# RWKV block products on all four 64 by 64 quarters of TensorE, with masks moved to GpSimd

## The reference

```
sa    = S @ a_t
S     = S * w_t + outer(sa, b_t) + outer(v_t, k_t)
y_t   = S @ r_t
```

## Time and profile before

| | us |
|---|---|
| median of 3 runs | 1494.84 |
| lowest and highest run | 1488.73, 1506.45 |
| profiled execution, its own time | 1494.61 |
| its span | 1492.7 |
| PE busy | 1369.0 (92%) |
| PEld busy | 1040.0 (70%) |
| DVE busy | 697.6 (47%) |
| ACT busy | 506.6 (34%) |
| POOL busy | 172.6 (12%) |

### The profile page before, as it was taken

How to read it: one execution, slowest core, us unless ns; L and a number is a source line. 1 busy time by engine, 2 the same in 40 slices (tenths; PEclk the granted TensorE clock), 3 DMA queues, 4 the chain that set the end, 5 groups by cost and what they waited for, 6 DMA issues and landing times.

```text
span 1492.7 us, 24385 instructions
## 1 busy us (share of the span) xinstructions
PE 1369.0 (92%) x10375; PEld 1040.0 (70%) x10375; DVE 697.6 (47%) x1097; ACT 506.6 (34%) x821; POOL 172.6 (12%) x76
## 2 busy tenths in 40 slices
PE   4998997998999999799997878899999999999995
PEld 3998997973689999698896867764444444444432
DVE  5764666534166666668984537441212212212113
ACT  2532333544343333357454132322222222222213
POOL 0000000000000000176881015400000000000000
PEclk8999999999999999999998998999999999999998
DMA  9755354229955544303416033408999999999992
GB/s 364 322 182 201 127 179 160 58 106 427 425 226 190 194 167 173 122 1 86 169 44 253 4 137 119 176 4 332 425 425 426 424 425 424 427 425 426 422 425 114
DMA packets 37505, 363.39 MB, mean 243 GB/s; under 512 B 5027, under 2 KB 6179, under 8 KB 8740
## 3 DMA queue, kind: packets, MB, share of 16 engines
q1 hardware_dynamic: 36692, 359.55, 60.0%
q0 software_dynamic: 720, 2.46, 0.8%
HBM read 359.30 MB, written 2.69 MB: 243 GB/s over the span
## 4 chain that ended last, share of the span: by engine, by line
PE 79%; DVE 12%; ACT 3%; DMA 3%; POOL 2%; issue 2%; DVEq 0%; SPq 0%; ACTq 0%
PE banks L1081 15%; PE banks L598 12%; PE banks L600 12%; PE banks L599 12%; PE banks L1106 8%; PE banks L1041 4%; PE banks L1032 4%; DMA ring<-ws 2%; PE banks L748 2%; POOL slot_lo L535 2%; PE banks L576 1%; PE banks L884 1%; PE banks L587 1%; PE banks L909 1%; PE banks L1047 1%
## 5 line engine op out<-in xcount | busy, mean ns | idle before, releaser
L598 PE MATMUL banks<-h_hi,gu_hi 128*128 128x256 f32 x704 | 200.8, 285 | 5.8 <-issue 5.8
L599 PE MATMUL banks<-h_lo,gu_hi 128*128 128x256 f32 x704 | 200.1, 284 | 0.0
L600 PE MATMUL banks<-h_hi,slot_lo 128*128 128x256 f32 x704 | 200.0, 284 | 0.0
L598 PEld LDWEIGHTS banks<-h_hi,gu_hi 128*128 128x128 f32 x704 | 136.2, 193 | 6.3 <-issue 6.2
L599 PEld LDWEIGHTS banks<-h_lo,gu_hi 128*128 128x128 f32 x704 | 136.1, 193 | 0.1
L600 PEld LDWEIGHTS banks<-h_hi,slot_lo 128*128 128x128 f32 x704 | 136.1, 193 | 0.0
L1967 DVE TENSOR_TENSOR out_lo<-banks,out_hi 128x512 fp32r<-128x512 f32 x64 | 44.3, 692 | 190.3 <-ACT out_hi L1446 190.3
L1106 PE MATMUL banks<-ring,scr 128*64 128x512 f32 x512 | 116.9, 598 | 1.9 <-ACT scr L1440 1.9
L600 PE MATMUL banks<-slot_lo,slot_lo 128*128 128x256 f32 x416 | 118.6, 285 | 0.0
L1081 PE MATMUL banks<-ring,scr 128*64 128x512 f32 x512 | 112.6, 592 | 0.0
L1081 PE MATMUL banks<-ring 128*64 128x512 f32 x512 | 112.6, 592 | 0.0
(11 more groups left out here) (401 smaller groups left out, 3066.7 us busy)
## 6 DMA issues: line engine op xcount, KB each, us to landing
ring<-ws SPq DMA_DIRECT2D x93, 1536.0 KB, 8.3
ring<-experts SPq DMA_DIRECT2D x64, 2048.0 KB, 9.9
ring<-experts SPq DMA_DIRECT2D x64, 1024.0 KB, 10.1
ring<-experts SPq DMA_DIRECT2D x1, 3072.0 KB, 10.8
scr<-bias_line POOLq DMA_DIRECT2D x4, 512.0 KB, 8.2
bias_line<-scr SPq DMA_DIRECT2D x1, 1536.0 KB
x<-xT SPq DMA_DIRECT2D x1, 1024.0 KB, 5.0
scr<-pool_w SPq DMA_DIRECT2D x1, 1024.0 KB, 7.6
```

The costliest lines, as they stand in the source:

```text
L598: nc.tensor.matmul(out, hi, move_hi, start=start, stop=False, skip_group_check=True)
L599: nc.tensor.matmul(out, hi, move_lo, start=False, stop=False, skip_group_check=True)
L600: return nc.tensor.matmul(out, lo, move_hi, start=False, stop=stop, skip_group_check=True)
```

## The change

The change lays out the block matrices anew. For an odd column block (heads 2, 3 and 6, 7) the rows that stand for tokens are put on the other half of the partitions (`token_rows(i, p)`: half p for even, half 1 - p for odd blocks), so that four products in a row (`i` and `p` in 0, 1) go to the four quarters. Blocks are numbered so that i is the highest part of the index (block 8 i + 2 c + x), and even and odd blocks write to different banks. Besides:

* GpSimd writes the identity into `inv` and `inv_t` in advance, and VectorE copies the first level's entries over it under a mask (`copy_predicated`), in place of a mask and an addition. For this a half set of 16 products more is made (L918 of the new file).
* The masks of levels 1 to 4 are made on GpSimd, as are those of `m_ak` and `m_rb`, which ScalarE copies out of PSUM first. VectorE keeps the masks of `m_ab`, of level 0 and of `m_rk`.
* `inv` and `inv_t` are signalled apart, and TensorE waits for each where it is read. Ahead of each half's X products it waits for the mask and for `inv`, and ahead of the corrections for the copy of X and for `inv_t`.
* In a chunk the next chunk's `m_ak` product is made before the state product; the output products come behind it, and the last chunk's state product is left out.

```diff
@@ -379,18 +379,44 @@
         LHALF = NCH * AC // 2
 
-        def level_bank(b0, half, col):
-
-            return banks[:, b0 + 2 * half:b0 + 2 * half + 2, col:col + LHALF // 2 * CH].rearrange("p a (j t) -> p a j t", t=CH)
-
         def level_half(a, half):
-            return a[:, half * LHALF:(half + 1) * LHALF, :].rearrange("p (j a) t -> p a j t", a=2)
+            return a.rearrange("p (i h s) t -> p i h (s t)", i=2, h=2)[:, :, half]
+
+        def x_banks(half):
+            return banks[:, 2 * half:2 * half + 2, 0:T]
+
+        def level_mask(n, half, dst, src, engine):
+            blocks = lambda a: a.rearrange("p (i h s) t -> p i h s t", i=2, h=2)[:, :, half]
+            return engine.tensor_tensor(blocks(dst), blocks(src), blocks(tile_masks("levels_t", CH * n)), ALU.mult)
...
@@ gpsimd
             for i in range(48):
                 second_part(i, win_lo_of(i), slot(S_WIN + i // 3)[:, win_tile(i)[1]], win_hi_of(i))
+            pool.wait_ge(proj_ready, U_Z + 48)
+            pool.wait_ge(tilde_ready, 1)
+            nc.gpsimd.tensor_copy(inv, tile_masks("eye")).then_inc(inv_ready, 1)
+            nc.gpsimd.tensor_copy(inv_t, tile_masks("eye")).then_inc(inv_ready, 1)
+            pool.wait_ge(pair_used, 1)
+            for n in range(1, len(LEVELS)):
+                for half in range(2):
+                    pool.wait_ge(level_x, 2 if n == 1 else 2 * (n - 1) + half + 1)
+                    level_mask(n, half, m_lev, m_ab, nc.gpsimd).then_inc(level_m, 1)
+            for n, (a, name) in enumerate(((m_ak, "strict_t"), (m_rb, "upto_t"))):
+                pool.wait_ge(turned_used, 4 + n)
+                nc.gpsimd.tensor_tensor(a, a, tile_masks(name), ALU.mult).then_inc(level_m, 1)
...
@@ tensor
-            def pairs(fn):
-
-                for i in range(NCH * AC):
-                    for p in range(2):
-                        c, hp = divmod((i + p * NCH * AC // 2) % (NCH * AC), AC)
-                        mm = fn(c, hp, slice(p * HEAD, (p + 1) * HEAD))
+            def half_rows(r):
+                return slice(r * HEAD, (r + 1) * HEAD)
+
+            def token_rows(i, p):
+                return half_rows(p ^ i)
+
+            def pairs(b0, fn):
+
+                for c in range(NCH):
+                    for x in range(2):
+                        for i in range(2):
+                            for p in range(2):
+                                n = (2 * c + x) * CH
+                                lhs, rhs = fn(2 * x + i, half_rows(p), slice(c * CH, (c + 1) * CH))
+                                mm = nc.tensor.matmul(B[b0 + i][token_rows(i, p), n:n + CH], lhs, rhs, start=True, stop=True, skip_group_check=True)
                 return mm
...
+            def level_x_products(half):
+                for n, lo, i, p in level_blocks(half):
+                    rows = token_rows(i, p)
+                    mm = nc.tensor.matmul(B[2 * half + i][half_rows(p), lo:lo + CH], m_lev[rows, n, :], inv[rows, n, :], start=True, stop=True, skip_group_check=True)
+                return mm
+
+            def level_inv_products(half):
+                for n, lo, i, p in level_blocks(half):
+                    rows = half_rows(p)
+                    mm = nc.tensor.matmul(B[2 * half + i][token_rows(i, p), T + lo:T + lo + CH], inv_t[rows, n, :], xm[rows, n, :], start=True, stop=True, skip_group_check=True)
+                return mm
+
+            def level_inv_t_products(half):
+                for n, lo, i, p in level_blocks(half):
+                    rows, lo = half_rows(p), i * T + lo
+                    mm = nc.tensor.matmul(B[4 + half][rows, lo:lo + CH], xm[rows, n, :], inv_t[rows, n, :], start=True, stop=True, skip_group_check=True)
                 return mm
 
             for n in range(len(LEVELS)):
                 for half in range(2):
-
+                    if n == 0:
+                        pe.wait_ge(pair_used, 4 + half)
+                    else:
+                        pe.wait_ge(inv_ready, adds_done(n - 1, half, False))
                     pe.wait_ge(level_m, 2 * n + half + 1)
-                    half_level(half, 0, 0, m_lev, inv).then_inc(level_x, 1)
+                    level_x_products(half).then_inc(level_x, 1)
                 for half in range(2):
+                    if n == 0:
+                        pe.wait_ge(turned_used, 4)
+                    else:
+                        pe.wait_ge(inv_ready, adds_done(n - 1, half, True))
                     pe.wait_ge(x_copied, 2 * n + half + 1)
                     if n < len(LEVELS) - 1:
-                        half_level(half, 4, 0, inv_t, xm)
-                    half_level(half, 4, T, xm, inv_t).then_inc(level_d, 1)
+                        level_inv_products(half).then_inc(level_d, 1)
+                    level_inv_t_products(half).then_inc(level_d, 1)
...
@@ vector
             dve.wait_ge(pair_ready, 1)
-            nc.vector.tensor_tensor(m_ab, pair_bank(6), every("strict_t"), ALU.mult).then_inc(pair_used, 1)
+            nc.vector.tensor_tensor(m_ab, pair_bank(6), tile_masks("strict_t"), ALU.mult).then_inc(pair_used, 1)
+            dve.wait_ge(inv_ready, INV_SET)
+            dve.wait_ge(pair_ready, 2)
+            nc.vector.copy_predicated(inv, tile_masks("first").bitcast(I32), pair_bank(0)).then_inc(pair_used, 1)
+            own_half = tile_masks("first_t", 0, 8).bitcast(I32)
+            nc.vector.copy_predicated(inv_t[:, 0:8, :], own_half, one_bank(6)).then_inc(pair_used, 1)
+            dve.wait_ge(pair_ready, 3)
+            nc.vector.copy_predicated(inv_t[:, 8:16, :], own_half, one_bank(2)).then_inc(pair_used, 1)
...
```

More of the change, by code:

```diff
@@ L875, in _ @@
-            pe.wait_ge(pair_used, 5)
-            def half_level(half, b0, col, stationary, moving):
-                for j in range(LHALF):
-                    for p in range(2):
-                        k, rows = j ^ p, slice(p * HEAD, (p + 1) * HEAD)
-                        n = half * LHALF + k
-                        lo = col + k // 2 * CH
-                        mm = nc.tensor.matmul(B[b0 + 2 * half + k % 2][rows, lo:lo + CH], stationary[rows, n, :], moving[rows, n, :], start=True, stop=True, skip_group_check=True)
+                pairs(2 * n, lambda hp, rows, t: (src[rows, hp, t], ident[rows, rows])).then_inc(turned, 1)
@@ new lines, in inner @@
+            def inner(lhs, rhs):
+                return lambda hp, rows, t: (lhs[rows, hp, t], rhs[rows, hp, t])
+            pairs(6, inner(b5, b4)).then_inc(pair_ready, 1)
+            pe.wait_ge(turned_used, 1)
+            pairs(0, inner(b4, b5)).then_inc(pair_ready, 1)
+            pe.wait_ge(turned_used, 2)
+            for c in range(NCH):
+                for d in range(2):
+                    for p in range(2):
+                        n, rows, t = (2 * c + d) * CH, half_rows(p), slice(c * CH, (c + 1) * CH)
+                        mm = nc.tensor.matmul(B[2][rows, n:n + CH], b5[rows, 2 * d + 1, t], b4[rows, 2 * d + 1, t], start=True, stop=True, skip_group_check=True)
@@ L905, in products @@
-            def products(b0, lhs, rhs, start, stop):
-                for hp, rows in halves:
-                    mm = nc.tensor.matmul(place(b0, hp, rows), lhs(hp, rows), rhs(hp, rows), start=start and hp % 2 == 0, stop=stop, skip_group_check=True)
-                return mm
+                        level_inv_products(half).then_inc(level_d, 1)
+                    level_inv_t_products(half).then_inc(level_d, 1)
+            pe.wait_ge(inv_ready, INV_DONE)
+            def products(b0, out_rows, lhs, rhs, start, stop):
+                for x in range(2):
+                    for i in range(2):
+                        for p in range(2):
+                            mm = nc.tensor.matmul(B[b0 + i][out_rows(i, p), x * CH:(x + 1) * CH], lhs(x, i, p), rhs(x, i, p), start=start and x == 0, stop=stop, skip_group_check=True)
+                return mm
@@ L1793, in _ @@
-            then(nc.vector.tensor_tensor(inv_t, m_ab, every("first_t"), ALU.mult))
-            then(nc.vector.tensor_tensor(inv_t, inv_t, every("eye"), ALU.add))
-            dve.wait_ge(pair_ready, 2)
-            nc.vector.tensor_tensor(inv, pair_bank(0), every("first"), ALU.mult).then_inc(pair_used, 1)
-            dve.wait_ge(pair_used, 2)
-            then(nc.vector.tensor_tensor(inv, inv, every("eye"), ALU.add))
-            for n, (dst, b0, m) in enumerate(((m_ak, 2, "strict_t"), (m_rb, 4, "upto_t"), (m_rk, 6, "upto_t"))):
-                dve.wait_ge(pair_ready, n + 3)
-                nc.vector.tensor_tensor(dst, pair_bank(b0), every(m), ALU.mult).then_inc(pair_used, 1)
@@ L1811, in _ @@
-                    last_level = n == len(LEVELS) - 1
-                    if not last_level:
-                        nc.vector.tensor_tensor(level_half(inv, half), level_half(inv, half), level_bank(4, half, 0), ALU.add)
-                    then(nc.vector.tensor_tensor(level_half(inv_t, half), level_half(inv_t, half), level_bank(4, half, T), ALU.add))
-                    if not last_level:
```

(5 more changed lines are left out.)

107 lines of the change are left out of this document (64 added, 43 removed).

## The result

The changed kernel takes 1483.81 us (median of 18 runs, 1473.7 to 1488.4) against 1493.3 (18 runs, 1486.52 to 1506.45): a ratio of 0.9941, 95% interval 0.9923 to 0.9959. The profiled execution has a span of 1485.7 us.

What follows compares the result with a forecast made beforehand. It took TensorE's record pace and its waits for VectorE and ScalarE in a 71.4 us stage as the bound; 9.2 + 12.6 + 3.7 - 0.4 = 25.1 us off 1494.61 gave 1469.6 us, range 1463 to 1487.

Steps and rivals of the forecast that it cites:

- the price of a record: TensorE's block products off the diagonal: four quarters at work take 14.6 ns a record, half of 29.2; bounds 13.3 and 29.2.
- the 0.4: Start of the attention, outside the stage: 0.4 us lost to the two identity copies on GpSimd.
- the unchanged pace: Rival's sum with records still at 29.2 ns: 15.9 us, levels 28.6, chunks 16.6 + 1.6; 1486.2 us in all; 12%.
- TensorE can't take in records faster than one per 27 ns: Rival on TensorE's front end: 27 ns is its sustained limit, stage part 60.1 us, 1483.3 us in all; 14%.
- a limit of intake holds for all: Sign separating two rivals: an intake limit slows all records, while a limit of shared rows spares the diagonal sets.
- quarters which share rows queue: Rival: a quarter's weight load waits for its row neighbour's matmul, so the pace stays 29.2 ns; 1486.2 us; 12%.
- GpSimd's masks: Rival in the levels: half masks, taken as 1.2 us, set the pace from 1.8 us; 1470 to 1485 us; 5%.
- The clock: Rival, slower: TensorE at 1.2 GHz for the whole stage, 4.2 us more than now, 1498.8 us; 5%.
- Before the levels: From the first turning product to the first X product: 9.1 us in place of 18.3, 9.2 less.
- The levels: The five levels of the inverse: 4.27 us a level against 7.05, 22.0 us in all against 34.6, 12.6 less.
- The chunks: First chunk product to head sums: 13.3 us against 18.6, of which the 1.6 "issue" wait is kept; 3.7 less.
- the sign of being wrong: Test for the whole stage: the forecast is wrong if any of its three parts saves less than half its term.

Runs made afterwards that it cites:

- the run on two quarters: The changed kernel with every head's token rows put back on its own half, so products use only the two diagonal quarters: 1479.45 us, ratio 0.9926.
- the looped turns: The changed kernel with TensorE's levels 1 to 3 as three turns of one loop: 1471.89 us, ratio 0.9844.
- the second execution: The changed kernel once more, the same text: 1479.47 us, ratio 0.9903, stage 61.01 us.
- the late load: The changed kernel with the shared expert's load asked for after the last chunk's output products instead of after the inverses: 1477.24 us, ratio 0.9904.
- the run without it: The changed kernel with the masks of levels 1 to 4 back on VectorE in place of GpSimd: 1480.85 us, ratio 0.9941.
- the version with all three: The changed kernel with block products merged to 128 columns, levels 1 to 3 looped and the shared expert's load moved later: 1472.66 us, ratio 0.9838.
- the run with X products twice: The changed kernel with every X product of the five levels issued twice into the same place, 320 records more: 1489.76 us, ratio 0.9998.

## Why the prediction was wrong

**The step that failed** is the price of a record: "With four quarters at work I take half of 29.2, 14.6 ns a record." For the array it is right, as 200 records in 3.15 us show. But the sum charges it for every record that isn't on the diagonal, as if TensorE always had its next instruction, and puts the supply of instructions at nothing. Where the code is straight, the supply sets 29 to 31 ns a record. The same error stands in the chunks: "Nothing in the change touches that wait, so I keep it." I had read 1.61 us of "issue" as a thing of its own, without asking what TensorE waits for when it waits for nothing. It was the one place in the stage where the supply had come out, beside the load. Everywhere else the array's 29.2 ns and the waits for VectorE left the instructions time to arrive; how narrowly, the run on two quarters shows. With the faster array there are eleven such waits, 14.7 us in all. Take them from 62.0 and 47.3 us are left; the forecast stage was 45.9 (71.4 less 25.5, the 0.4 being elsewhere), and 44.3 without the 1.6 of "issue" in it.

The sum that would have held stood among the rivals. At the unchanged pace it gives 15.9, 28.6 and 18.2 us, 62.7 in all; the run on two quarters has 15.91, 27.94 and 19.91. So the rest of the change was priced well, and what was wrong is what the quarters add to it.

**The rivals.** None of them was it. The one nearest to it, that TensorE can't take in records faster than one per 27 ns, had the right height (59.7 us for the stage, against 62.0 and 61.0) for the wrong reason: 200 records have been taken in at 15 ns, until those fetched ahead were used up. That its 27, the supply's 29 to 31 and the old 29.2 ns lie so close is chance. Its test as I wrote it ("a limit of intake holds for all") would have shown it right to a reader of averages, since the stops fall on all products alike. The Trainium skill ("TensorE: Matmul & The Clock Gate", Part 1, on the 56 ns) puts the floor at about 25 ns; the 15.2 ns of 1209 records speaks against that for quarters. That quarters which share rows queue is wrong by the same rows. GpSimd's masks took 1.26 us where 1.2 was assumed, and were never waited for. The clock did fall, but behind the stop beside the load, and not in the stage at large. The 0.4 us that I counted for the identity copies elsewhere is less than these whole times can tell.

**The terms.** *Before the levels*: 13.8 and 13.2 us in place of 9.1, so 4.5 to 5.0 less instead of 9.2; three stops of 1.28, 1.80 and 1.57. The masked copies were right (1.28 and 0.71 against 1.24 and 0.65). *The levels*: 4.3 to 5.4 less instead of 12.6; the mechanism is right, as the looped turns of 4.32 us show, and the size is not, at some 5.9 us a level. *The chunks*: 0.6 less, in the second execution none, instead of 3.7. In the profiled execution all three save less than half of their terms, which the prediction gave as the sign of being wrong. With the late load they are 13.90 long, 13.3 by the forecast and without the 1.6 that I had kept.

**Where the 9.4 us came from.** The run on two quarters gives it: from 71.44 to 63.76, 7.7 us, is what the rest of the change did, and 2.3 us is what the four quarters added (to the mean of 61.5, and executions of one text lie 1 us apart). I had the shares the other way round, some 9 and 17. In the old levels VectorE's three operations a half stood in the chain twice, 3.9 us beside TensorE's 3.1; with a wait for each half's sums apart TensorE streams all the time, 5.67 us for 7.05. The masks' move to GpSimd had no part in it that the run without it shows. Which of the others had how much, the identity in advance or the finer waits, was not taken apart.

## What to carry to other kernels

Where an engine waits for "issue" in a stage of many short instructions, count them, divide by the time and look for the instruction queue's packets. A bound just below the present one looks like nothing until the present one goes. Before making such instructions faster, make them fewer, by wider operands or by a loop whose body is fetched once, and keep large loads out of the stage. Then measure the faster array again: the same edit was worth 2 us with the supply in the way and 14 where it was relieved (in a version whose wider products gain more from it, and with 1.9 us of clock in the 14).

## What the runs showed of the hardware

TensorE's instructions came in packets of 16 KB, 256 instructions. Where it ran out of them it went on every 3.4 to 4.3 us, 3.7 to 4.0 in the mean of a run: 29 to 31 ns for a record of two. Some 400 instructions (200 records, once 195) lay ready at the start of a straight stretch. Loops of 128, 384 and 768 instructions ran without such stops once their first turn was over.

Four f32 quarters of 64x64 ran at 14.7 to 17 ns a record; two at 29.2. With 128 columns it was 27 ns (1.75 us for 64, in the version with all three) against 55 (3.50 us).

Beside a load of 3 MB the four-quarter stream of the changed kernel stopped for 2.9 to 3.3 us, where its other stops were at most 1.9, and the packets lay 7.25 and 7.5 us apart. The clock fell to 0.50 behind these stops and behind that of 2.06 us on two quarters, and stayed at 1.00 behind the one of 1.61 us. It also fell without one: in the run with X products twice it was 0.50 from 871 to 873, and TensorE had been busy 1.02 of the 2 us from 866 and 1.07 of the 2 from 868, with no gap over 1.2 us. With 8 columns a product, busy all the time, TensorE was granted 0.50 to 0.53.
